# Two-block fp32 transformer layer on one core: the SSD decay rows of each head pair come to the partitions by DMA from a DRAM scratch, not by selector matmuls, and the minimum touches the diagonal blocks only

## The reference

```python
x = xh * dt[..., None]                       # 32 heads of 64, 256 tokens, one chunk
a_cs = cumsum(dt * a)                        # one row of 256 numbers for each head
decay = exp(where(causal, a_cs[l] - a_cs[s], -inf))
cb = einsum("bclgn,bcsgn->bcgls", cc, bc)    # C B^T, one 256x256 for each of 4 groups
y_diag = einsum("bcgrls,bcsgrp->bclgrp", cb * decay, x)
y = (y_diag + xh * d_skip) * silu(z)         # then grouped rmsnorm, then w_out
```

## Time and profile before

| | |
|---|---|
| median of three runs | 2723.26 us (2709.26 to 2724.82) |
| profiled execution, first to last instruction | 2709.7 us |
| TensorE busy | 99% |
| VectorE busy | 72% |
| ScalarE busy | 48% |
| DMA engines busy | about 55% |
| granted TensorE clock | 0.999 |

### The profile page before, as it was taken

The page is one execution under the profiler, slowest core; times in us unless marked ns, Lnnn a source line. Parts: engine busy times, 40 slices in busy tenths (PEclk is TensorE's granted clock), DMA queues, the critical chain, the costliest instruction groups (busy, mean ns, idle before and its releaser), DMA issues.

```text
span 2709.7 us, 37303 instructions
## 1 busy us (share of the span) xinstructions
PE 2695.0 (99%) x15244; PEld 2330.3 (86%) x15244; DVE 1949.2 (72%) x2419; ACT 1302.7 (48%) x1664; POOL 96.0 (4%) x68
## 2 busy tenths in 40 slices
PE   9999999999999999999999999999999999999998
PEld 7888888888898888888888888888888888888887
DVE  8777888986868665666566776777787757775775
ACT  5444556755545443444344554645544433443444
POOL 2000000012101000000000120000000000000000
PEclk9999999999999999999999999999999999999999
DMA  7555555456556655555555555454555565565554
GB/s 241 189 186 186 179 171 171 148 177 213 190 170 195 211 189 194 189 191 188 192 188 187 194 187 179 148 171 148 178 181 195 192 193 180 186 203 194 177 192 159
DMA packets 140058, 501.48 MB, mean 185 GB/s; under 512 B 15456, under 2 KB 18800, under 8 KB 139632
## 3 DMA queue, kind: packets, MB, share of 16 engines
q1 hardware_dynamic: 136512, 491.15, 54.8%
q10 hardware_dynamic: 3376, 7.96, 0.9%
HBM read 496.93 MB, written 3.68 MB: 185 GB/s over the span
## 4 chain that ended last, share of the span: by engine, by line
PE 94%; DVE 3%; ACT 2%; issue 0%; DMA 0%; POOL 0%; SPq 0%; DVEq 0%; ACTq 0%
PE PS L514 94%; DVE wlo L1302 1%; ACT whi L865 1%; DVE AR L1661 0%; DVE AR L1432 0%; ACT AR L971 0%; ACT L850 0%; DVE AR L1439 0%; DMA XG<-in_x 0%; DVE AR L1285 0%; DVE AR L1448 0%; DVE H L1296 0%; ACT AR L850 0%; DVE AR L1442 0%; PE PS L762 0%
## 5 line engine op out<-in xcount | busy, mean ns | idle before, releaser
L514 PE MATMUL PS<-H,whi 128*128 128x512 f32 x5072 | 1781.6, 396 | 3.3 <-DVE wlo L1302 2.0
L1302 DVE TENSOR_TENSOR wlo<-raw,whi 128x1024 fp32r<-128x1024 f32 x929 | 1136.7, 1241 | 598.0 <-ACT whi L865 596.5
L865 ACT ACTIVATE whi<-raw 128x1024 fp32r<-128x1024 f32 x929 | 973.6, 1057 | 954.4 <-PE PS L514 879.3
L514 PE MATMUL PS<-H,wlo 128*128 128x256 f32 x5072 | 1411.1, 278 | 0.0
L514 PEld LDWEIGHTS PS<-H,whi 128*128 128x128 f32 x5072 | 952.0, 188 | 228.6 <-issue 8.3
L514 PEld LDWEIGHTS PS<-H,wlo 128*128 128x128 f32 x5072 | 955.2, 188 | 2.5 <-issue 1.9
L514 PE MATMUL PS<-Y,whi 128*128 128x512 f32 (+1 forms) x1408 | 473.6, 387 | 0.8 <-DVE XG L1797 0.5
L514 PE MATMUL PS<-Y,wlo 128*128 128x256 f32 x1344 | 373.9, 278 | 0.0
L514 PEld LDWEIGHTS PS<-Y,whi 128*128 128x128 f32 x1408 | 260.0, 188 | 58.5 <-issue 1.7
L514 PEld LDWEIGHTS PS<-Y,wlo 128*128 128x128 f32 x1344 | 253.0, 188 | 0.3
L514 PE MATMUL PS<-whi,Y 128*128 128x512 f32 x704 | 216.6, 389 | 0.0
(11 more groups left out here) (200 smaller groups left out, 1095.1 us busy)
## 6 DMA issues: line engine op xcount, KB each, us to landing
raw<-in_ffn SPq DMA_DIRECT2D x528, 512.0 KB, 4.5
raw<-in_w_in SPq DMA_DIRECT2D x177, 512.0 KB, 4.5
raw<-in_w_qkv SPq DMA_DIRECT2D x96, 512.0 KB, 3.7
raw<-in_w_out SPq DMA_DIRECT2D x64, 512.0 KB, 4.5
raw<-in_w_o SPq DMA_DIRECT2D x40, 512.0 KB, 3.6
raw<-in_w_q SPq DMA_DIRECT2D x8, 512.0 KB, 4.5
raw<-in_w_k SPq DMA_DIRECT2D x8, 512.0 KB, 4.1
raw<-in_w_v SPq DMA_DIRECT2D x8, 512.0 KB, 4.2
```

The source lines that it names most:

```text
L514: return e.matmul(out, l, r, start=start, stop=stop)
L865: a.then_inc(e.activation(c.whi[:, s % NW, :], c.raw[:, s % NRAW, :], ACT.Copy), "whi")
L1302: v.then_inc(e.tensor_tensor(c.wlo[:, s % NW, :], c.raw[:, s % NRAW, :], c.whi[:, s % NW, :].bitcast(F32), ALU.subtract), "wlo")
```

## The change

For the row of each head, the selector products, their PSUM banks and waits, `SEL`, the lower half of `ACS` and task `cr` go. After the rows are made (now one copy, fp32, 32 partitions), ScalarE writes them to a DRAM scratch `acs_rows` of 32 x 384. For each pair, SP issues two transfers that read one row of the scratch 128 times over into the pair's E tiles, 192 KB each. They stand in SP's order behind chosen weight loads. VectorE's minimum works in place on the E tile, on its two diagonal blocks only (256 columns in place of 384). The E tiles rotate over four buffer pairs. Three semaphores of transfers and copies are merged with others.

```diff
-    "ssd": [("b0", 0, 2, "ssd_min", 2, 1), ("b1", 0, 2, "ssd_min", 2, 2), ("o", 0, 3, "ssd_z", 1, 1)],
+    "ssd": [("o", 0, 3, "ssd_z", 1, 1)],
...
-        self.ssd_e = [(G[3], G[4]), (G[5], M[0]), (M[1], M[2])]
+        self.ssd_e = [(G[1], G[2]), (G[5], M[0]), (M[1], M[2]), (G[3], G[4])]
...
+    def rows(i):
+
+        s.wait_ge("acs", 16)
+        if i > 3:
+            s.wait_ge("ssd_pv", i - 3)
+        elif i == 1:
+            s.wait_ge("dt_v", 6)
+        elif i == 2:
+            s.wait_ge("dt_v", 6)
+            s.wait_ge("xs_turn", 7)
+        elif i == 3:
+            s.wait_ge("xbc_conv", 12)
+        for n, h in enumerate((2 * i, 2 * i + 1)):
+            src = c.acs_rows[h:h + 1].to_broadcast([P, 384])
+            e.dma_start(c.ssd_e[i % 4][n][:, 0:384], src).then_inc(c.sems[f"row{i % 4}"], 16)
+
+    rows_at = {}
+    for i in range(16):
+        rows_at.setdefault((first_slot("z") + 4 * i + 1 - 12 * (i < 2) - 4 * (i == 2)) // 2 + 9, []).append(i)
     for w in range(4, N_SUB):
         load(w)
+        for i in rows_at.get(w, ()):
+            rows(i)
...
-        row = bank[0:64, 128:384]
-        for o in (0, 32):
-            mm(row[o:o + 32, :], c.adt[:, 0:32], c.tri[:, 0:256], True, False)
-        for o in (0, 32):
-            last = mm(row[o:o + 32, 128:256], c.adt[:, 32:64], c.tri[:, 0:128], False, True)
+        row = bank[0:32, 128:384]
+        mm(row, c.adt[:, 0:32], c.tri[:, 0:256], True, False)
+        last = mm(row[:, 128:256], c.adt[:, 32:64], c.tri[:, 0:128], False, True)
...
     def ssd(i):
-        p.wait_ge("dt_v", 6)
-        p.wait_ge("cr", 4)
-        for n, h in enumerate((2 * i, 2 * i + 1)):
-            bank = take("ssd", i, f"b{n}")
-            p.then_inc(mm(bank[:, 0:384], c.SEL[:, h:h + 1].to_broadcast([P, P]), c.ACS, True, True), "ssd_dec")
         yield from idle(SSD_PV[i % 2])
...
+        e.dma_start(c.acs_rows, c.ACS).then_inc(c.sems["acs"], 16)
...
     def ssd(i):
         yield from idle(1)
         v.wait_ge("xbc_conv", 12)
-        v.wait_ge("ssd_pv", i - 2) if i > 2 else None
+        v.wait_ge(f"row{i % 4}", 32 * (i // 4) + 32)
         for n, h in enumerate((2 * i, 2 * i + 1)):
-            E, bank = c.ssd_e[i % 3][n], c.bank("ssd", i, f"b{n}")
-            v.wait_ge("ssd_dec", 2 * i + n + 1)
-            own = c.acs[:, 3 * h:3 * h + 3].unsqueeze(2).to_broadcast([P, 3, P])
-            v.then_inc(e.tensor_tensor(three(E), three(bank[:, 0:384]), own, ALU.min), "ssd_min")
+            diag = three(c.ssd_e[i % 4][n])[:, 0:3:2, :]
+            own = c.acs[:, 2 * h:2 * h + 2].unsqueeze(2).to_broadcast([P, 2, P])
+            v.then_inc(e.tensor_tensor(diag, diag, own, ALU.min), "ssd_min")
```

More of the change, by code:

```diff
@@ L329 @@
 SEMS = (
-    "pe_own act_own dve_own pool_own raw0 raw1 raw2 raw3 x0 x1 x2 x3 x4 x5 x6 x7 c1 raw_first whi_first wlo_first scaled vec mem c2 rel rel_row rows bias masked out "
-    "whi wlo sub_done acc0 acc1 h_hi h_made y_hi y_made cr "
+    "pe_own act_own dve_own pool_own raw0 raw1 raw2 raw3 x0 x1 x2 x3 x4 x5 x6 x7 c1 raw_first whi_first wlo_first scaled vec mem c2 rel_row rows bias masked out "
+    "whi wlo sub_done acc0 acc1 h_hi h_made y_hi y_made "
     "sq sum_add sum_half norm_sum norm_mean norm_root norm_ok "
-    "msq madd mnorm_sum mnorm_mean mnorm_root mnorm_ok mcol_turn mcol_ok rcol_turn rcol_ok "
-    "x_first sc_sq sc_sum sc_root sc_gain sc_v xbc_low xbc_conv xbc_silu cb_mm cb_copy dt_v dt_a dt_p dt_pos dt_log acs_hi xs_turn xs_copy z_made z_silu "
-    "ssd_dec ssd_min ssd_exp cb_mask ssd_e ssd_pv ssd_z grp_sq grp_add grp_sum grp_root grp_y "
+    "msq madd mnorm_sum mnorm_mean mnorm_root mnorm_ok col_turn mcol_ok rcol_ok "
+    "x_first sc_sq sc_sum sc_root sc_gain sc_v xbc_low xbc_conv xbc_silu cb_mm cb_copy dt_v dt_a dt_p dt_pos dt_log acs xs_turn xs_copy z_made z_silu "
+    "row0 row1 row2 row3 ssd_min ssd_exp cb_mask ssd_e ssd_pv ssd_z grp_sq grp_add grp_sum grp_root grp_y "
     "xa_s xa_max xa_exp xa_w xa_turn xa_copy xa_pv xqk qk ffn_gate ffn_up ffn_conv ffn_silu "
@@ L351, in __init__ @@
         self.d, self.out = d, out
-        sb("gap", [P, 96])
+        sb("gap", [P, 128])
         self.raw = sb("raw", [P, NRAW, SUB])
@@ L538, in mcol @@
     def mcol(_):
-        column("mcol", 0, c.RMB, "mnorm_ok", 1, "mcol_turn")
+        column("mcol", 0, c.RMB, "mnorm_ok", 1, "col_turn")
         yield
     def rcol(_):
-        column("rcol", 0, c.RN, "rr", 1, "rcol_turn")
+        column("rcol", 0, c.RN, "rr", 1, "col_turn")
         yield
@@ L610, in ssd @@
         for n, h in enumerate((2 * i, 2 * i + 1)):
-            E = c.ssd_e[i % 3][n]
+            E = c.ssd_e[i % 4][n]
             o = bank[64 * n:64 * n + 64, 0:T]
@@ L950, in dt @@
         yield from idle(4)
-        row = c.bank("dt", 0, "n")[0:64, 128:384]
+        row = c.bank("dt", 0, "n")[0:32, 128:384]
         a.wait_ge("dt_p", 2)
-        a.then_inc(e.activation(c.ACS[0:64, 0:256], row, ACT.Copy))
-        a.then_inc(e.activation(c.ACS[0:64, 256:384], row[:, 128:256], ACT.Copy), "acs_hi")
+        a.then_inc(e.activation(c.ACS[:, 0:256], row, ACT.Copy))
+        a.then_inc(e.activation(c.ACS[:, 256:384], row[:, 128:256], ACT.Copy), "dt_log")
+        yield
+        a.wait_ge("dt_log", 2)
+        a.wait_ge(*a.at)
+        e.dma_start(c.acs_rows, c.ACS).then_inc(c.sems["acs"], 16)
         yield
@@ L1413, in dt @@
         bank = c.bank("dt", 0, "n")
-        v.wait_ge("acs_hi", 1)
+        v.wait_ge("dt_log", 2)
         v.wait_ge("dt_log", 1)
         v.then_inc(e.scalar_tensor_tensor(c.nacs, bank[:, 0:64], -1.0, c.ldt, ALU.mult, ALU.add))
[L1417 to L1421, removed]
+        for b in range(2):
+            v.then_inc(e.tensor_copy(c.acs[:, b:64:2], bank[:, 32 * b:32 * b + 32]), "dt_v" if b else None)
         yield
@@ L1810, in follow @@
                 lo(MADE[version][0], k, 1, c.xt(k), c.gain(gain, k))
[L1812 to L1818, removed]
     side = Side({"norm": norm, "mnorm": mnorm, "mcol": mcol, "rcol": rcol, "mem": mem, "sc": sc, "cb": cb, "dt": dt, "ssd": ssd, "grp": grp,
[L1821 removed]
+                 "xa": xa, "const": const, "qa": qa, "mid": mid, "dfa": dfa, "dfb": dfb, "stk": stk, "bnd": bnd})
     v.then_inc(e.memset(c.warm, 0.0))
```

21 lines of the change are left out of this document (12 added, 9 removed).

## The result

The changed kernel takes 2736.45 us (median), the kernel before in the same call 2711.23 us. The ratio is 1.0065 (1.0046 to 1.0083), slower by less than the 1% that I took as the bound of no change. The forecast was 2723.2 us with a range of 2709 to 2733, and the time lies above it.

A forecast was written before the change was run, and what follows sets the result against it. VectorE's loop with ScalarE was taken to set the SSD stage's end: late rows +1.0, first cycle -0.3, last stretch -0.8, sum -0.1 us on the 2709.7 span; plus 13.6 from span to median gave 2723.2 us, range 2709 to 2733.

The follow-up runs named there:

- e3: Changed kernel with the row transfers of pairs 3 to 15 issued one weight load earlier; 2717.79/2732.23 us (lower/upper group), ratio to before 1.0036.
- e5: Changed kernel with rows of pairs 3 to 15 one load earlier and tensors at the old addresses; 2708.45/2722.06 us (lower/upper group), ratio to before 0.9993.
- e11: e5 with one spare matmul 16 slots into the first feed-forward part; 2709.23 us, all 11 runs in the lower group, ratio to before 0.9995.
- e8: Changed kernel with one more spare matmul 16 slots into the second feed-forward part; 2734.56 us, one group only, ratio to before 1.0075.
- e1: Kernel before with only SEL moved ahead of raw, so raw to CR stand 128 bytes higher; 2720.69/2734.66 us (lower/upper group), ratio to before 1.0051.
- e6: Changed kernel with raw, whi and wlo at the old addresses, only H, Y and CR 128 bytes higher; 2743.31 us, one group only, ratio to before 1.0106.
- e2: Changed kernel with tensors at the old addresses (gap 96 columns, pad of 32 behind CR); 2715.53/2728.93 us (lower/upper group), ratio to before 1.0002.

## What to carry over

A transfer that must arrive on time behind another on one queue should be priced from the slowest neighbour in the same queue and issued one load earlier than that asks; the step cost nothing here (e3). When a diff moves tensors by so much as a pad, that is a change of its own: hold the addresses still, or time the pad alone, before the rest is judged. And where a kernel's times come in two groups, compare group with group, and know to which one a profiled run belongs. Of a stage, compare the length: its start alone moved by 1.65 us between two runs of the same program up to there (e5, e11).

## What the runs showed of the hardware

- A stream of matmuls without a wait, at clock 1.00, ran at 347, 351 or 353 ns a block pair by rhythm, 1.8% apart. Over this kernel that is 9 to 28 us. By the Trainium skill, "TensorE: Matmul & The Clock Gate", section "Back-to-back issue gap", 512 and 256 columns take 215.8 and 109.2 ns alone, an estimate of 325 a pair; no run here came to that, and the difference between the rhythms isn't in it.
- The rhythm can change at a single matmul of another kind and was kept until the next (e8), and 128 bytes in the place of stationary and moving data change which one follows (e1, 9.7 us; e6, 28 us above e2's lower group). The two groups of times, 14 us apart, are the first feed-forward part in one rhythm or the other, which falls out one way or the other from run to run: in the traces of all eleven kernels that have both groups the count goes with the group, x2309, x2307 and x2310 in those of before, e2 and e5 (lower), x2265, x2266 and x2266 in those of after, e1 and e3 (upper). The odds aren't the same in each call: before had 17 of 31 runs in the upper group in one and none of 27 in another. What decides it is open.
- Busy time showed none of it, 100% in each window of before, after and e1; the count of matmuls in equal windows did.
- A row of DRAM spread over 128 partitions (192 KB) on SP, behind a load of 512 KB, landed 3.8 to 6.7 us after issue. Such a row issued by ScalarE took 3.3 to 4.4.
